# Last two up columns of an expert layer taken together, gated sums folded in at columns 124 and 125, residual loaded at column 70

## The reference

```python
def _peer(h, w_q, subkeys, w_down, w_up):
    ...
        v, i = lax.top_k(s, PEER_TOPK)
    ...
        u = w_down[eidx]
        a = jax.nn.gelu(jnp.einsum('btd,btpkd->btpk', hblk, u).astype(jnp.float32))
        vv = w_up[eidx]
        return jnp.einsum('btpk,btpkd->btd', (w * a).astype(hblk.dtype), vv)
...
        h = _modulate(_rms_norm(x, g_norm_ffn[l]), sh2, sc2)
        x = x + ga2[:, None, :] * _peer(h, w_peer_q[l], peer_subkeys[l], peer_down[l], peer_up[l])
    return _rms_norm(x, g_norm_final)
```

## Time and profile before

| | us |
|---|---|
| median of three runs | 1203.29 |
| the runs | 1199.77 to 1206.89 |
| the profiled execution's own time | 1205.66 |
| its span | 1203.9 |
| PE busy in it | 1141.1 (95%) |
| DVE / POOL / ACT busy | 886.1 / 719.5 / 617.4 |

### The profile page before, as it was taken

One profiled execution on the slowest core, in us unless ns is written; L12 is line 12 of the kernel. 1 busy time (PEld: TensorE's weight loads), 2 busy tenths in 40 slices (PEclk: granted clock), 3 DMA queues, 4 the chain that ended last, 5 costly groups with the idle time before them and its releaser, 6 DMA issues.

```text
span 1203.9 us, 18849 instructions
## 1 busy us (share of the span) xinstructions
PE 1141.1 (95%) x6904; PEld 987.6 (82%) x6904; DVE 886.1 (74%) x1762; ACT 617.4 (51%) x1186; POOL 719.5 (60%) x451
## 2 busy tenths in 40 slices
PE   4999999999998999999999999999999999899995
PEld 2778877777776799999999999999977767677884
DVE  5678666587878652999665666666588889898886
ACT  1545444453554444445565656555564545455563
POOL 0886759674443202888777777798665766465600
PEclk9999999999999999999999999999999999999998
DMA  9988774445341441565555555576579999999975
GB/s 375 420 328 338 278 293 161 184 166 207 143 158 71 177 173 36 186 194 196 188 168 184 169 176 184 176 260 193 177 248 347 357 331 333 340 346 342 351 265 156
DMA packets 68332, 282.06 MB, mean 234 GB/s; under 512 B 10384, under 2 KB 10768, under 8 KB 55952
## 3 DMA queue, kind: packets, MB, share of 16 engines
q1 hardware_dynamic: 56544, 246.54, 57.6%
q0 software_dynamic: 11264, 33.60, 7.6%
q10 hardware_dynamic: 432, 0.72, 0.2%
HBM read 274.53 MB, written 6.29 MB: 233 GB/s over the span
## 4 chain that ended last, share of the span: by engine, by line
PE 70%; DVE 11%; DMA 9%; issue 4%; ACT 3%; POOL 2%; SPq 0%; DVEq 0%; POOLq 0%; ACTq 0%
PE bank L1649 10%; PE bank L1653 10%; PE bank L1650 10%; DMA ring<-in_up 8%; PE banks L1243 3%; PE banks L1249 2%; PE bank L1243 2%; PE bank L1249 2%; PE bank L1255 2%; PE banks L1255 2%; DVE banks L2315 2%; PE banks L1663 2%; DVE split_r L2328 2%; PE banks L1702 1%; PE bank L1697 1%
## 5 line engine op out<-in xcount | busy, mean ns | idle before, releaser
L845 POOL TENSOR_TENSOR split_r<-ring,split_r 128x1024 fp32r<-128x1024 f32 x128 | 307.9, 2406 | 137.2 <-ACT split_r L911 137.1
L911 ACT ACTIVATE split_r<-ring 128x1024 fp32r<-128x1024 f32 x192 | 203.3, 1059 | 232.1 <-PE bank L1653 171.8
L1649 PE MATMUL bank<-h_high_r,split_r 128*128 128x256 f32 x1024 | 251.4, 283 | 0.7 <-issue 0.7
L1650 PE MATMUL bank<-h_low_r,split_r 128*128 128x256 f32 x1024 | 251.2, 283 | 0.0
L1649 PEld LDWEIGHTS bank<-h_high_r,split_r 128*128 128x128 f32 x1024 | 196.5, 192 | 0.9 <-ACT G L1081 0.9
L1650 PEld LDWEIGHTS bank<-h_low_r,split_r 128*128 128x128 f32 x1024 | 196.5, 192 | 0.0
L798 POOL TENSOR_TENSOR wq_low_r<-G,G_r 128x512 fp32r<-128x512 f32 (+1 forms) x104 | 134.9, 1331 | 48.5 <-ACT G_r L906 48.5
L829 POOL DMA_INDIRECT G<-in_up,tab x64 | 93.4, 1460 | 87.2 <-DVE banks L2315 71.6
L1653 PE MATMUL bank<-h_high_r,split_r 128*128 128x256 f32 x1024 | 143.7, 283 | 0.0
L1653 PEld LDWEIGHTS bank<-h_high_r,split_r 128*128 128x128 f32 x1024 | 132.1, 192 | 0.0
L798 POOL TENSOR_TENSOR wq_low_r<-G,hT_r 128x512 fp32r<-128x512 f32 x48 | 63.2, 1351 | 57.2 <-ACT hT_r L906 57.2
(11 more groups left out here) (477 smaller groups left out, 2581.2 us busy)
## 6 DMA issues: line engine op xcount, KB each, us to landing
ring<-in_down SPq DMA_DIRECT2D x128, 512.0 KB, 3.6
ring<-in_up SPq DMA_DIRECT2D x128, 512.0 KB, 5.7
G<-in_ada SPq DMA_DIRECT2D x32, 1024.0 KB, 10.6
G<-in_in SPq DMA_DIRECT2D x32, 1024.0 KB, 7.2
G<-in_out SPq DMA_DIRECT2D x8, 1024.0 KB, 7.1
G<-in_wq SPq DMA_DIRECT2D x8, 1024.0 KB, 7.8
z_few<-G SPq DMA_DIRECT2D x16, 256.0 KB, 2.2
tab<-in_ada SPq DMA_DIRECT2D x4, 1024.0 KB, 8.3
```

The source lines that it names most:

```text
L845: pool.tensor_tensor(wsplit[:, j % SPLIT, 1, :], raw[:, j % RAW, :], wsplit[:, j % SPLIT, 0, :].bitcast(F32), ALU.subtract).then_inc(low_r ...
L911: nc.scalar.activation(split_parts(n)[:, 0, :], raw[:, n % RAW, :], ACT.Copy).then_inc(high_ready, 1)
L1649: mm(o, w[0][:, c, :], h_high[:, c, :], start=(c == 0), stop=False)
L1650: mm(o, w[0][:, c, :], h_low[:, c, :], start=False, stop=False)
```

## The change

Three places of the program are rewritten, and no matmul is added or left out.

- SP: the four loads of x_back and the one of gfin2 are issued behind the ring load of column 74 (at n = P + RAW + 70), no longer behind the last one.
- PE: `last_two` takes columns 126 and 127 together. First the eight matmuls of both for the mixed tile, column 127's low part last, then six for the first half of the pure tile and six for the second. It waits for the high parts of both columns, for gs and for column 126's low part ahead of the first matmul.
- DVE: the second half of the gathered sums is added at column 123 in place of 124; at 124 the lanes 64 to 127 of `few` are multiplied with the gate; at 125 they are added to x_back, and gfin2 gets its factor. Behind the loop the mixed tile's three operations work on lanes 0 to 63 only. ACT's moves no longer wait for `few_added`.

The diff:

```diff
--- before.py
+++ after.py
@@ -759,6 +759,12 @@
                     m = (n - RAW + 1) // STAGE - 1
                     sp.wait_ge(gelu_done, STAGE * (m + 1))
                     sp.dma_start(z_few[:, m * STAGE:(m + 1) * STAGE, :], stage[:, m % 2]).then_inc(z_stored[m % 2], 16)
+                if n == P + RAW + 70:
+                    sp.wait_ge(col_done, P + 64)
+                    sp.wait_ge(x_saved, 16)
+                    for t, lane, at, src in TAIL_ROWS:
+                        sp.dma_start(x_back[lane:lane + FEW, t, :], out[at:at + FEW, src, :]).then_inc(x_reloaded, 16)
+                    sp.dma_start(gfin2, d["gfin2"].partition_broadcast(P)).then_inc(x_reloaded, 16)
                 if n - RAW - P in GATE_LOAD:
                     k = GATE_LOAD.index(n - RAW - P)
                     if k == 0:
@@ -767,11 +773,6 @@
                         sp.wait_ge(gate_step, 4 * k)
                     half = slice((k % 2) * 2048, (k % 2 + 1) * 2048)
                     sp.dma_start(tab[:, 0:2048], d["ada2"][10 + k // 2][:, half]).then_inc(gate_in, 16)
-            sp.wait_ge(col_done, P + 64)
-            sp.wait_ge(x_saved, 16)
-            for t, lane, at, src in TAIL_ROWS:
-                sp.dma_start(x_back[lane:lane + FEW, t, :], out[at:at + FEW, src, :]).then_inc(x_reloaded, 16)
-            sp.dma_start(gfin2, d["gfin2"].partition_broadcast(P)).then_inc(x_reloaded, 16)
             for k, (t, half) in enumerate(LATE_ORDER):
                 c = slice(half * 512, (half + 1) * 512)
                 sp.wait_ge(out_ready, k + 1)
@@ -1157,7 +1158,6 @@
                     nc.scalar.activation(gs[k % 2][:, :, 0:TD], Gv[:, part, :], ACT.Copy)
                     nc.scalar.activation(gs[k % 2][:, :, TD:TD + FEW], Gv[:, part, 0:FEW], ACT.Copy).then_inc(gs_high, 1)
 
-            act.wait_ge(few_added, 2)
             for half in range(2):
                 c = slice(half * 512, (half + 1) * 512)
                 act.wait_ge(sum_done, half + 1)
@@ -1708,24 +1708,35 @@
                     pe_.wait_ge(gate_step, 8 * (k + 1))
                     mm(ps[k][:, :], ones, gate_acc[k], start=True, stop=True).then_inc(gate_full, 1)
 
-            def last_up(n):
-
-                first, both, first_low, w, halves = up_parts(n)
-                pe_.wait_ge(gs_high, n // GS_GROUP + 1)
-                pe_.wait_ge(high_ready, P + n + 1)
-                pe_.wait_ge(gs_low, n // GS_GROUP + 1)
+            def last_two(n):
+
+                parts = [up_parts(m) for m in (n, n + 1)]
+                pe_.wait_ge(gs_high, (n + 1) // GS_GROUP + 1)
+                pe_.wait_ge(high_ready, P + n + 2)
+                pe_.wait_ge(gs_low, (n + 1) // GS_GROUP + 1)
                 wait_up_low(pe_, n)
+                first, both, first_low, w, halves = parts[0]
+                for part in range(2):
+                    for half, cols in halves:
+                        mm(ps[6 + half][:, :], both, w[:, part, cols], start=False, stop=False, skip_group_check=True)
+                first, both, first_low, w, halves = parts[1]
                 for half, cols in halves:
                     mm(ps[6 + half][:, :], both, w[:, 0, cols], start=False, stop=False, skip_group_check=True)
+                wait_up_low(pe_, n + 1)
+                for half, cols in halves:
                     mm(ps[6 + half][:, :], both, w[:, 1, cols], start=False, stop=True, skip_group_check=True).then_inc(sum_done, 1)
-                for half, cols in halves:
-                    mm(ps[4 + half][:, :], first, w[:, 0, cols], start=False, stop=False, skip_group_check=True)
-                    mm(ps[4 + half][:, :], first_low, w[:, 0, cols], start=False, stop=False, skip_group_check=True)
-                    mm(ps[4 + half][:, :], first, w[:, 1, cols], start=False, stop=True, skip_group_check=True).then_inc(sum_done, 1)
-
-            for n in range(P - 1):
+                for half in range(2):
+                    for m in range(2):
+                        first, both, first_low, w, halves = parts[m]
+                        cols = halves[half][1]
+                        mm(ps[4 + half][:, :], first, w[:, 0, cols], start=False, stop=False, skip_group_check=True)
+                        mm(ps[4 + half][:, :], first_low, w[:, 0, cols], start=False, stop=False, skip_group_check=True)
+                        ins = mm(ps[4 + half][:, :], first, w[:, 1, cols], start=False, stop=(m == 1), skip_group_check=True)
+                    ins.then_inc(sum_done, 1)
+
+            for n in range(P - 2):
                 up(n)
-            last_up(P - 1)
+            last_two(P - 2)
 
 
         @block.vector
@@ -2339,30 +2350,36 @@
                 if n == FOLD_COLUMN:
                     dve.wait_ge(row_used, FEW)
                     nc.vector.tensor_copy(few[FEW:P, :], row_sum[0:FEW, :]).then_inc(few_added, 1)
-                if n == FOLD_COLUMN + 2:
+                if n == FOLD_COLUMN + 1:
                     dve.wait_ge(few_added, 1)
                     tt(few[FEW:P, :], few[FEW:P, :], row_sum[FEW:P, :], ALU.add).then_inc(few_added, 1)
-
-            dve.wait_ge(x_reloaded, 16 * 5)
-            link(ts(gfin2, gfin2, ROOT_D, None, ALU.mult))
-            dve.wait_ge(gate_added, 2)
-            dve.wait_ge(few_added, 2)
+                    dve.wait_ge(gate_added, 2)
+                if n == FOLD_COLUMN + 2:
+                    dve.wait_ge(few_added, 2)
+                    tt(few[FEW:P, :], few[FEW:P, :], gateB[FEW:P, :], ALU.mult).then_inc(few_added, 1)
+                if n == FOLD_COLUMN + 3:
+                    dve.wait_ge(few_added, 3)
+                    dve.wait_ge(x_reloaded, 16 * 5)
+                    tt(x_back[FEW:P, 1, :], x_back[FEW:P, 1, :], few[FEW:P, :], ALU.add).then_inc(few_added, 1)
+                    ts(gfin2, gfin2, ROOT_D, None, ALU.mult).then_inc(few_added, 1)
+
+            dve.wait_ge(few_added, 5)
 
             def add_sum(k):
 
                 t, half = LATE_ORDER[k]
                 c = slice(half * 512, (half + 1) * 512)
                 dve.wait_ge(sum_done, k + 1)
+                lanes = slice(0, FEW if t == 1 else P)
+                src = ps[(6 if t == 1 else 4) + half][lanes, :]
                 if t == 1:
                     dve.wait_ge(few_moved, half + 1)
-                    tt(few[0:FEW, c], ps[6 + half][0:FEW, :], few[0:FEW, c], ALU.add).then_inc(few_added, 1)
-                    dve.wait_ge(few_added, half + 3)
-                    src = few[:, c]
-                else:
-                    src = ps[4 + half][:, :]
-                tt(fin[:, t, c], src, gateB[:, c], ALU.mult).then_inc(gated, 1)
+                    tt(few[lanes, c], src, few[lanes, c], ALU.add).then_inc(few_added, 1)
+                    dve.wait_ge(few_added, half + 6)
+                    src = few[lanes, c]
+                tt(fin[lanes, t, c], src, gateB[lanes, c], ALU.mult).then_inc(gated, 1)
                 dve.wait_ge(gated, k + 1)
-                tt(x_back[:, t, c], x_back[:, t, c], fin[:, t, c], ALU.add).then_inc(y2_ready, 1)
+                tt(x_back[lanes, t, c], x_back[lanes, t, c], fin[lanes, t, c], ALU.add).then_inc(y2_ready, 1)
 
             def variance(k, t):
```

## The result

| | before | changed |
|---|---|---|
| median, 22 runs each | 1207.35 us | 1213.24 us |
| lowest to highest | 1199.77 to 1213.61 | 1208.87 to 1219.06 |
| the profiled execution's own time (span) | 1205.66 (1203.9) | 1211.86 (1210.0) |

The ratio is 1.0050, with a 95% interval of 1.0035 to 1.0066: **6.0 us slower**, where +4.0 was forecast. The 22 runs of before lie 4 us above the three on which the forecast stood, so the measured 1213.24 us is outside the range of 1201 to 1212. The direction was right and the size too small. Of 35 runs of the kernel before on another chip one took 1878.73 us, and the ratios leave it out.

A forecast was written before the change was run, and what follows sets the result against it. PE was taken as the bound, DMA close behind. Part 1's +3.5 us and +0.54 us for Part 2 and Part 3 together made +4.0, against 1203.29 us giving 1207.3 us; range 1201.0 to 1212.0.

The forecast's parts named there:

- Part 1: Reload moved to column 70: column 75's ring load queues behind it, PE stalls 3.3 us; with corrections +3.5 us.
- two samples: Ring loads issued behind 1024 KB gate loads, used 9.55 and 8.45 us later: 3.3 us on average over the median 5.7.
- In proportion: Scaling the 3.3 us delay for 1024 KB to the reload's 1536 KB, giving 5.0 us.
- the cover: Slack of column 75 before PE is late, 1.67 us, taken off the 5.0 us delay.
- The corrections: After column 75's stall: +1 us for late following columns, -0.8 us for later PE losses that DMA working ahead removes.
- rival 2: PE's clock falls at one of the two new stalls, column 75 or the end: +8 us, 1211.3 us; chance 0.22.
- Rival 1: Reload bytes fit into DMA's free time at column 70, column 126's split on time: 1202.2 us; chance 0.20.
- Part 2: Columns 122 to 127: 3.13 us more DVE work ahead of column 126's split, which ends at 1186.54; columns 124, 125 covered.
- Part 3: Last two columns together: new 1.67 us stall at column 126, mixed tile's half five matmuls earlier; +0.54 us with Part 2.
- The signs: Profile checks: ACT wait over 3 us, PE idle 2 to 5 at column 75, 1.3 to 2.1 before 126, tail 14.8.
- The last one: Check for the whole forecast: time from column 70 to the end should be 3 to 5 us longer.

The follow-up runs named there:

- reload70_only: Kernel before with only the five reloads (x_back and gfin2) moved to one burst at column 70, the end as it was; ratio 1.0046 to the kernel before.
- busy75: Changed kernel with five unread matmuls into a free bank on PE ahead of column 75's wait; one run, no ratio, loss 8.8 us over columns 68 to 82.
- wide70: Changed kernel with x_back loaded at column 70 by two 128-lane DMAs instead of four of 64 lanes, gfin2 as it is; ratio 1.0027 to the kernel before.
- narrow_spread: As wide_spread, with each 512 KB x_back load cut into two 64-lane loads of 256 KB at the same places; ratio 1.0045 to the kernel before.
- wide_spread: Changed kernel with the reload as three 128-lane loads of 512 KB at columns 70, 74 and 78; ratio 0.9998 to the kernel before.
- burst112: Changed kernel with the same burst of five reloads at column 112 instead of 70; ratio 1.0038 to the kernel before.
- late_reload: Changed kernel with its five reloads issued one by one at columns 110 to 118 instead of at 70; ratio 1.0004 to the kernel before.
- gfin70: Changed kernel with only gfin2's 512 KB at column 70 and x_back's loads at 112; one run, no ratio, loss 2.8 us over columns 68 to 82.

## Why the prediction was wrong in size

**Part 1, column 75's lateness: the term that failed.** The mechanism was right and the stall mis-sized. It was put at 3.3 us, from two samples per KB (3.3 us for 1024 KB, 5.0 for 1536). Column 75 started 4.2 and 4.1 us late in the two profiles of the changed kernel, 5.1 in reload70_only and 4.3 in busy75. Two things are missing from the term.

- *The rate.* "In proportion" priced x_back's loads as if they were gate loads of 128 lanes. They move 230 GB/s, not 400: 1024 KB take 4.6 us and not 2.6. The row for it was in the trace of before (229 and 238 GB/s at a share of over 1), in the stretch in which the reload itself ran, and wasn't read; I read its issue times and not its rate.
- *SP's own time.* The prediction read the 2.49 + 0.58 us of issue and put them at nothing: it left column 75's ring load "issued at 1056.36 now". It went out 2.1 us behind its free slot.

With 128 lanes and three DMAs, in wide70, both are small, and the stall was 3.4 and 4.0 us: there the 3.3 us nearly hold. Inside a burst no run parts the rate from the issue time, and together they are worth less than either price, some 0.8 us. Outside a burst narrow_spread against wide_spread shows the rate's cost (the two differ in the lanes and, with them, in two loads of 256 KB for one of 512). The 3.3 us also hold a slip that helped: the 5.0 us of delay are counted over a median of 5.7 us, and the cover over column 75's own 6.3 us (1056.36 to 1062.63). On one base the forecast would have been a stall of some 2.8 us.

**The corrections, and rival 2.** +1 for followers and -0.8 for gaps won back made +0.2. From column 75's start to column 82's the loss was 2.6 and 2.5 us against 1.8 without a burst, so +0.7 or +0.8; nothing was won back later (means of 3.7 us from column 82 to 125 with and without a burst). The sum of part 1 was to be +3.5; the measured loss over the mean of 2.8 is 5.1 and 5.0. In it column 75 ran at 1.2 GHz for most of its length, 1.7 and 1.6 us over 2.27. That was rival 2, given 0.22; the fall came after 4.05 us of idle time, as it came after 1.92 in burst112 and 2.32 in late_reload. The rival's price of 1.7 us is right for the column and wrong for the stretch, as busy75 shows. Its condition doesn't fit its price either: used 9 us behind its issue, column 75 would start 9 - 6.3 - 1.7 = 1.0 us late and not 4.7. And 4.7 + 1.5 + 1.7 + 0.54 is 8.4 and not 8.

**Rival 1** (the bytes fit in) did not come, though gfin70 shows that it would have, for 512 KB alone.

**Part 2, DVE's queue: right.** Column 126's split was to end 3.13 us later than without the new operations, and to be what PE waits for. The stall of 1.44 us (forecast 1.67) was ended by that split.

**Part 3: right in its mechanism, 0.5 us too high.** +0.54 was forecast, +0.05 seen in the profile, and -0.3 in the second profile (18.5 us against 18.8); the mean of twelve profiles with this end is -0.2, late_reload's with its lower clock at +2.3 left aside. 0.2 us of it is the shorter stall, 0.35 the move behind the seventh matmul (below). The ratio of reload70_only, without the new end, is the same as the changed kernel's within the intervals. 14.8 us from DVE's first sum on stood, as did the cover of columns 124 and 125 and of the tail's reload.

**The signs.** Those named at the start of the change and at column 126 came: ACT's wait of 6.78 us, PE's 4.05 at column 75, 1.44 between columns 125 and 126 with DVE's split behind it, 14.8 us to the end. The last one failed: from column 68 to the end the changed kernel took 8.5 us longer and not 3 to 5. Of this 5.6 are the reload's stretch and 2.8 the chance of the later columns, which no term of the forecast had.

**The level.** The forecast in microseconds stood on three runs (1199.77 to 1206.89). Twenty-two gave 1207.35. A range that took in what three runs leave open, some 3 us either way, would have held the time.

## What to carry to other kernels

Before a DMA is moved into a stretch whose loads are on the path, read at what rate that very transfer runs (GB/s at a full share), not only its size: a load of 64 lanes held DMA for as long as one of nearly twice its bytes at 128 lanes. Read also how long the queue's engine takes to issue it, since the loads behind it wait for that too. Then cut it to what the ring's cover hides, here 512 KB at full rate every four columns; the same bytes in one burst cost 5 us, even where DMA was a quarter idle. A stall of 2 us and more on PE has to be priced with the clock's fall behind it, which here came more often than not; but what the fall costs is read from what comes next. It was 1.8 us where the next columns' data were there, and little where they were late themselves.
